# Down projection of the context rows in plain fp32 on four column quarters of the array

## The reference

```python
def expert_choice_ffn(x, w_router, w_gate, w_up, w_down):
    ...
    g, idx = lax.top_k(aff, cap)
    xs = jax.vmap(lambda xb, ib: xb[ib])(x, idx)
    hcur = jax.nn.silu(jnp.einsum('becd,edf->becf', xs, w_gate)) * jnp.einsum('becd,edf->becf', xs, w_up)
    ys = jnp.einsum('becf,efd->becd', hcur, w_down) * g[..., None].astype(x.dtype)
    return jax.vmap(lambda yb, ib: jnp.zeros((n, D), yb.dtype).at[ib.reshape(-1)].add(yb.reshape(-1, D)))(ys, idx)
```

## Time and profile before

| | |
|---|---|
| Median of 3 runs | 3972.54 us (3972.15 to 3976.68) |
| Profiled execution, its own time | 3971.88 us |
| Its span | 3970.1 us |
| Granted TensorE clock, mean | 0.975 |
| Busy PE, PEld, DVE, ACT, POOL | 95%, 85%, 62%, 45%, 12% |
| Expert stage | from about 2200 to 3895 us |

### The profile page before, as it was taken

One profiled execution on the slowest core, in us unless ns is written; L12 is line 12 of the kernel. 1 busy time (PEld: TensorE's weight loads), 2 busy tenths in 40 slices (PEclk: granted clock), 3 DMA queues, 4 the chain that ended last, 5 costly groups with the idle time before them and its releaser, 6 DMA issues. The chain is left out here.

```text
span 3970.1 us, 63525 instructions
## 1 busy us (share of the span) xinstructions
PE 3764.5 (95%) x22936; PEld 3367.7 (85%) x22936; DVE 2455.5 (62%) x4637; ACT 1774.2 (45%) x2654; POOL 472.3 (12%) x517
## 2 busy tenths in 40 slices
PE   8999999999989999999987899999999999999992
PEld 4799999999988888888876788888888888888981
DVE  4745555555566666332225677777777777777774
ACT  3611111111367776311104666666666666665653
POOL 0000000000264644010101000000000000000000
PEclk9999999999999999999998899999999999999996
DMA  9434434433654645645317587888788778888886
GB/s 378 146 129 138 137 124 137 137 130 131 187 168 137 203 144 173 258 144 215 139 40 298 186 259 259 266 264 262 255 275 259 254 261 264 262 263 265 264 251 249
DMA packets 556531, 825.31 MB, mean 208 GB/s; under 512 B 24320, under 2 KB 426144, under 8 KB 544672
## 3 DMA queue, kind: packets, MB, share of 16 engines
q1 hardware_dynamic: 532384, 702.27, 53.4%
q0 software_dynamic: 24064, 121.93, 9.4%
HBM read 717.18 MB, written 108.00 MB: 208 GB/s over the span
## 5 line engine op out<-in xcount | busy, mean ns | idle before, releaser
L2159 DVE TENSOR_TENSOR e_wlo<-e_raw,e_whi 128x1024 fp32r<-128x1024 f32 x768 | 905.2, 1219 | 327.2 <-ACT e_whi L2078 323.9
L2296 PE MATMUL ps<-e_xs,e_whi 128*128 128x320 f32 x4096 | 1054.8, 344 | 10.0 <-DVE e_xs L2173 6.9
L2296 PE MATMUL ps<-e_xs,e_wlo 128*128 128x160 f32 x4096 | 934.9, 238 | 0.0
L2078 ACT ACTIVATE e_whi<-e_raw 128x1024 fp32r<-128x1024 f32 x768 | 766.0, 1049 | 284.8 <-DMA e_raw<-in_w_down 106.4
L2296 PEld LDWEIGHTS ps<-e_xs,e_wlo 128*128 128x128 f32 x4096 | 770.3, 191 | 0.7
L2296 PEld LDWEIGHTS ps<-e_xs,e_whi 128*128 128x128 f32 x4096 | 752.8, 188 | 14.4 <-issue 7.3
L2314 PE MATMUL ps<-e_whi,e_h 128*128 128x512 f32 x1024 | 403.1, 394 | 0.9 <-DVE e_h L2199 0.9
L531 PE MATMUL ps<-hhi,p_whi 128*128 128x428 f32 (+1 forms) x1536 | 381.8, 357 | 8.4 <-DVE p_wlo L463 8.4
L481 DVE SCALAR_TENSOR_TENSOR p_acc<-p_modraw,cT,p_acc 128x256 f32<-128x256 f32 x960 | 386.6, 478 | 0.3 <-DMA p_modraw<-in_w_mod 0.3
L531 PE MATMUL ps<-hlo,p_whi 128*128 128x428 f32 (+1 forms) x1536 | 382.4, 357 | 0.0
L531 PE MATMUL ps<-hhi,p_wlo 128*128 128x428 f32 (+1 forms) x1536 | 380.3, 356 | 0.0
(11 more groups left out here) (252 smaller groups left out, 5359.0 us busy)
## 6 DMA issues: line engine op xcount, KB each, us to landing
e_raw<-in_w_gate SPq DMA_DIRECT2D x64, 2048.0 KB, 7.9
e_raw<-in_w_up SPq DMA_DIRECT2D x64, 2048.0 KB, 7.8
e_raw<-in_w_down SPq DMA_DIRECT2D x64, 2048.0 KB, 8.0
p_modraw<-in_w_mod SPq DMA_DIRECT2D x128, 512.0 KB, 3.5
m_raw<-in_w_mod SPq DMA_DIRECT2D x16, 2048.0 KB, 13.3
p_raw<-in_w_in SPq DMA_DIRECT2D x64, 512.0 KB, 4.7
o_raw<-in_w_out SPq DMA_DIRECT2D x16, 2048.0 KB, 9.0
projT<-p_out_st POOLq DMA_DIRECT2D x30, 640.0 KB, 3.8
```

The costliest lines, as they stand in the source:

```text
L2078: nc.scalar.activation(piece(whi, c, q), piece(raw, c, q), ACT.Copy).then_inc(w_hi_made, 1)
L2159: nc.vector.tensor_tensor(piece(wlo, c, q), piece(raw, c, q), piece(whi, c, q).bitcast(F32), ALU.subtract).then_inc(w_lo_made, 1)
L2296: last = nc.tensor.matmul(bank[:, 0:cols], w[:, s, at:at + P], xs[:, k, 0:cols], start=(k == 0 and w is whi), stop=(k == KD - 1 and w is whi))
```

## The change

The context rows' down product is made by plain fp32 matmuls: h_ctx holds the 32 context rows of h unsplit, and the moving operand is raw itself. Feature block k goes to column quarter k % 4 of the array, that is, to output partitions 32 (k % 4) and up, so that bank 5 or 7 ends with four partial sums. ScalarE copies the first into ys_c (copy_first_part), VectorE adds the other three (SUMS counts the steps of the semaphore, NPART is 4). The h tile keeps only latent columns.

The 8 matmuls of a chunk are a call of ctx_rows. Chunks 0 and 1 are called after feature block 3 of chunk 0, chunk 2 after block 5 of chunk 1, chunk 3 after block 5 of chunk 2. A call waits for all 8 blocks of h, for the chunk's weights in raw and for the scaling that frees its bank. Since raw has a second reader, pieces of wlo wait for the calls, and with them the loads.

```diff
-                sp.wait_ge(w_lo_made, e * EP + c * NP + NP)
+                sp.wait_ge(w_lo_made, e * EP + c * NP + (NP + 3 if c == NUP + 2 else NP))
...
-                nc.scalar.activation(h[:, 2 * j + b, 0:CAP], usum[:, b, :], ACT.Copy).then_inc(h_hi, 1)
-
-            def copy_ctx_low(e, d):
-
-                act.wait_ge(piece_used, e * EP + (NUP + d) * NP + NP + SLOTS)
-                nc.scalar.activation(ctx_low[:, d % 2, :], ps[CAP_C:2 * CAP_C, 5 + (d % 2) * 2, :], ACT.Copy
-                                     ).then_inc(ctx_low_copied, 1)
+                nc.scalar.activation(h[:, 2 * j + b, 0:CAP_L], usum[:, b, 0:CAP_L], ACT.Copy).then_inc(h_hi, 1)
+
+            def copy_first_part(e, d):
+
+                act.wait_ge(ctx_multiplied, e * ND + d + 1)
+                if d == 0:
+                    act.wait_ge(scattered, e * 32 + FIRST)
+                nc.scalar.activation(ys_c[:, d * DW:d * DW + DW], ps[0:CAP_C, 5 + (d % 2) * 2, :], ACT.Copy
+                                     ).then_inc(first_part_copied, 1)
...
                 for q in pieces:
+                    if c == NUP + 1 and q == 2:
+                        dve.wait_ge(ctx_multiplied, e * ND + 1)
+                    if c % NCH > NUP and c < NCH and q == 3:
+                        dve.wait_ge(ctx_multiplied, e * ND + (c - NUP + 1))
...
-                nc.vector.tensor_tensor(h[:, 2 * j + b, CAP:CAP + CAP_C], full[:, CAP_L:CAP], hi[:, CAP_L:CAP],
-                                        ALU.subtract)
+                nc.vector.tensor_copy(h_ctx[:, 2 * j + b, :], full[:, CAP_L:CAP])
...
-                dve.wait_ge(ctx_low_copied, e * ND + d + 1)
-                nc.vector.tensor_tensor(ys_c[:, cols], ps[0:CAP_C, bank + 1, :], ctx_low[:, d % 2, :], ALU.add
-                                        ).then_inc(ctx_summed, 1)
-                dve.wait_ge(ctx_summed, e * ND + d + 1)
+                dve.wait_ge(first_part_copied, e * ND + d + 1)
+                for part in range(1, NPART):
+                    nc.vector.tensor_tensor(ys_c[:, cols], ps[part * CAP_C:part * CAP_C + CAP_C, bank + 1, :],
+                                            ys_c[:, cols], ALU.add).then_inc(affinity_or_ctx_sum, 1)
+                    dve.wait_ge(affinity_or_ctx_sum, e * SUMS + 2 + d * (NPART - 1) + part)
...
+            def ctx_rows(e, d):
+
+                c = NUP + d
+                pe.wait_ge(h_lo, e * KF + KF)
+                pe.wait_ge(w_loaded[c % 2], e * (NCH * 8) + (c // 2) * 16 + 16)
+                pe.wait_ge(ys_made, e * (2 * ND) + (2 * (d - 1) if d >= 2 else 0) + AHEAD)
+                bank = 5 + (d % 2) * 2
+                for k in range(KF):
+                    part = k % NPART
+                    last = nc.tensor.matmul(ps[part * CAP_C:part * CAP_C + CAP_C, bank, :], h_ctx[:, k, :],
+                                            raw[:, c % 2, k * DW:k * DW + DW], start=(k < NPART),
+                                            stop=(k >= KF - NPART))
+                last.then_inc(ctx_multiplied, 1)
...
-                            parts = [(h[:, k, CAP_L:CAP + CAP_C], wh, 2 * CAP_C), (h[:, k, CAP_L:CAP], wl, CAP_C)]
-                            for x, w, rows in parts if k < KF - 1 else parts[::-1]:
-                                last = nc.tensor.matmul(bc[0:rows, :], x, w, start=(k == 0 and w is wh),
-                                                        stop=(k == KF - 1 and w is wh))
+                                last = nc.tensor.matmul(bl, x, w, start=(k == 0 and i == 0),
+                                                        stop=(k == KF - 1 and i == 2))
                             if k % 2 == 1:
                                 last.then_inc(piece_used, 1)
+                            if d == 0 and k == 3:
+                                ctx_rows(e, 0)
+                                ctx_rows(e, 1)
+                            if d in (1, 2) and k == 5:
+                                ctx_rows(e, d + 1)
```

More of the change, by code:

```diff
@@ L1953, in experts @@
     TURNS = (range(0, 2), range(2, NGR))
+    NPART = P // CAP_C
+    SUMS = 2 + ND * (NPART - 1)
     XSTEPS = NGR + 1
@@ L1971, in experts @@
     ys_made = sem("e_ys_made")
-    affinity_set = sem("e_affinity_set")
     scattered = sem("e_scattered")
-    ctx_low_copied = sem("e_ctx_low_copied")
-    ctx_summed = sem("e_ctx_summed")
+    first_part_copied = sem("e_first_part_copied")
+    ctx_multiplied = sem("e_ctx_multiplied")
+    affinity_or_ctx_sum = sem("e_affinity_or_ctx_sum")
     with ExitStack() as ctx:
@@ L1985, in experts @@
         usum = sb("e_usum", [P, 2, CAP])
-        h = sb("e_h", [P, KF, 2 * CAP], F32R)
+        h = sb("e_h", [P, KF, 2 * CAP_L], F32R)
         ys_c = sb("e_ys_c", [CAP_C, D])
-        ctx_low = sb("e_ctx_low", [CAP_C, 2, DW])
+        h_ctx = sb("e_h_ctx", [P, KF, CAP_C])
         index_l = sb("e_index_l", [P, 1], U32)
@@ L2131, in expert @@
                     else:
-                        copy_ctx_low(e, c - NUP - 1)
+                        copy_first_part(e, c - NUP - 1)
                     if following:
@@ L2139, in expert @@
                             ctx_high(e + 1)
-                copy_ctx_low(e, ND - 1)
+                copy_first_part(e, ND - 1)
             make_hi(0, 0, range(NP))
@@ L2195, in h_low @@
                 dve.wait_ge(h_hi, e * KF + 2 * j + b + 1)
-                hi, full = h[:, 2 * j + b, 0:CAP].bitcast(F32), usum[:, b, :]
-                nc.vector.tensor_tensor(h[:, 2 * j + b, CAP:CAP + CAP_C], full[:, CAP_L:CAP], hi[:, CAP_L:CAP],
-                                        ALU.subtract)
-                nc.vector.tensor_tensor(h[:, 2 * j + b, CAP + CAP_C:2 * CAP], full[:, 0:CAP_L], hi[:, 0:CAP_L],
+                hi, full = h[:, 2 * j + b, 0:CAP_L].bitcast(F32), usum[:, b, :]
+                nc.vector.tensor_copy(h_ctx[:, 2 * j + b, :], full[:, CAP_L:CAP])
+                nc.vector.tensor_tensor(h[:, 2 * j + b, CAP_L:2 * CAP_L], full[:, 0:CAP_L], hi,
                                         ALU.subtract).then_inc(h_lo, 1)
@@ L2235, in expert @@
                         dve.wait_ge(scattered, e * 32 + FIRST)
-                        nc.vector.tensor_copy(aff_l[:], gL[:, ds(e, 1)]).then_inc(affinity_set, 1)
-                        nc.vector.tensor_copy(aff_c[:], gC[0:CAP_C, ds(e, 1)]).then_inc(affinity_set, 1)
-                        dve.wait_ge(affinity_set, e * 2 + 2)
+                        nc.vector.tensor_copy(aff_l[:], gL[:, ds(e, 1)]).then_inc(affinity_or_ctx_sum, 1)
+                        nc.vector.tensor_copy(aff_c[:], gC[0:CAP_C, ds(e, 1)]).then_inc(affinity_or_ctx_sum, 1)
+                        dve.wait_ge(affinity_or_ctx_sum, e * SUMS + 2)
                     else:
@@ L2302, in expert @@
                         d = c - NUP
-                        bl, bc = (ps[:, 4 + (d % 2) * 2, :], ps[:, 5 + (d % 2) * 2, :])
+                        bl = ps[:, 4 + (d % 2) * 2, :]
                         pe.wait_ge(ys_made, e * (2 * ND) + (2 * (d - 1) if d >= 2 else 0) + AHEAD)
@@ L2311, in expert @@
                             wh, wl = (w[:, s, k * DW:k * DW + DW] for w in (whi, wlo))
-                            hh, hl = h[:, k, 0:CAP_L], h[:, k, CAP + CAP_C:2 * CAP]
+                            hh, hl = h[:, k, 0:CAP_L], h[:, k, CAP_L:2 * CAP_L]
                             for i, (x, w) in enumerate(((hh, wh), (hh, wl), (hl, wh))):
-                                nc.tensor.matmul(bl, x, w, start=(k == 0 and i == 0), stop=(k == KF - 1 and i == 2))
-                            parts = [(h[:, k, CAP_L:CAP + CAP_C], wh, 2 * CAP_C), (h[:, k, CAP_L:CAP], wl, CAP_C)]
-                            for x, w, rows in parts if k < KF - 1 else parts[::-1]:
-                                last = nc.tensor.matmul(bc[0:rows, :], x, w, start=(k == 0 and w is wh),
-                                                        stop=(k == KF - 1 and w is wh))
+                                last = nc.tensor.matmul(bl, x, w, start=(k == 0 and i == 0),
+                                                        stop=(k == KF - 1 and i == 2))
                             if k % 2 == 1:
                                 last.then_inc(piece_used, 1)
+                            if d == 0 and k == 3:
[3 more added lines that the diff above has]
+                                ctx_rows(e, d + 1)
                         if d < 2 and not last_expert:
```

## The result

The changed kernel takes 4240.28 us (median, 4233.61 to 4244.75), the kernel before on the same chip 3972.35 (3969.18 to 3976.68): ratio 1.0669, 95% interval 1.0656 to 1.0683, so 268 us or 16.7 us per expert slower. The profiled execution took 4233.61 us.

The account below looks back on a forecast made before the run. PE was taken to set the pace, 104.5 us per expert, 16 times. The profiled execution's 3971.9 plus 256 us (16.0 per expert, work and waits) plus 62 us of clock gave 4290 us; range 4120 to 4425.

Parts of the forecast that it names:

- rival (a): Context calls: four quarters really run together, 1.7 us a call; 4129 us, or 4170 with clock loss; chance 0.28.
- Removed: Down part on PE: two of five 512-column matmuls go, 14.7 us per expert.
- Added on PE: Context calls: plain fp32 matmuls overlapping in a chain, 3.9 us per chunk, 15.5 per expert; switches 0.6 more.
- The wait for h: Before the first context call: PE waits for all 8 h blocks, 5.9 us per expert (3.9 to 6.3).
- The two for the scaling: Third and fourth context calls: PE waits for VectorE's scaling to free the bank, 4.9 and 2.4 us per expert.
- The start of the next expert: Second gate/up block: VectorE's pieces come late for PE, some 1.8 us more per expert.
- Clock: PE at half speed after the 5.9 and 4.9 us waits, second counted half: 3.9 us per expert, 62 us.
- Rival (d): Expert stage: waits as worked out, but the clock does not fall; 4228 us; chance 0.11.
- (b): Context calls: no overlap at all, 6.9 us a call; 4378 us, or 4420 with clock loss; chance 0.22.
- (c): Down part: quarters together and waits mostly absent; faster if waits total below 7.2 us per expert, at best 3857; chance 0.04.
- starts nearly together in fours: Profile sign in the context calls: instructions starting this way would mean four quarters really run together.
- VectorE's total still fits. Its order does not: VectorE: 80.2 of 104.5 us per expert, so its total fits, but its order makes PE wait.

Follow-up runs that it names:

- without the scatter: Changed kernel with the two transfers adding an expert's rows to y replaced by two one-row transfers: 4200.53 us, ratio 1.0568.
- The filled waits: Changed kernel plus unread matmuls, 14 before the first context call and 26 before the third (none there in the last expert): 4198.79 us, ratio 1.0563.
- the one-quarter run: Changed kernel with all eight matmuls of a context call in column quarter 0: 4478.12 us, ratio 1.1276.
- the order mended: Changed kernel with the down chunks' scaling and sums put ahead of the next block's first two pieces: 4147.18 us, ratio 1.0442.
- no block held, the calls late and one addition: Changed kernel with calls reading context inputs instead of raw, first two calls after the last h block, one VectorE addition per chunk: 3973.43 us, ratio 1.0005.

## Why the prediction was right

Forecast 4290, measured 4240.28, inside the range and inside the forecast's own 4220 to 4340. That it fell into the latter was luck: PE's work was put 7.8 us per expert too high, the waits 1.7 and the clock 2.5 too low. The true case was rival (a), whose waits add up to 17.0 us (5.9 + 7 + 2.2 + 1.9) against 16.7 measured; its 4170 is too low because it counts 2.6 us of clock where there were 6.4. Per expert, for the 16.7 us:

**Removed**, 14.7 us of PE: as forecast. PE's busy time is nearly the same as before (3759.9 against 3764.5) only because half clock puts back what the shorter work saves.

**Added on PE**: here the step failed. "The second of quarter 0 starts with the first of quarter 1, and so on down the chain" gave 3.9 us per call; it is 1.9 at full clock. That puts PE's work at 4 x 1.92 + 0.6 - 14.7 = 6.4 us less, where the forecast had 1.4 more. The quarters' disjoint outputs, which I named as the only thing for rival (a), were enough. Beside it I had set a rule, that starts and ends keep program order across tiles (the Trainium skill, TensorE: Matmul & The Clock Gate, Part 3). It gives 3.9 us only if the two instructions of a matmul are neighbours in that order, which was my assumption; the rows show 1.92. Whether the rule or the assumption fails is open, since no row here shows which instruction of a pair starts when.

**Waits**: right in kind and place, wrong in size. The wait for h is 4.1 us (65.9 over 16; forecast 5.9, bounds 3.9 to 6.3). The two for the scaling make 9.0 (143.3 over 16; forecast 4.9 + 2.4, in (a) 7 + 2.2). The start of the next expert costs 3.6 more (61.5 - 3.2, over 16; forecast 1.8). The forecast has no term for the load that takes some 12 us beside the scatter; without the scatter 1.4 of the 3.6 go (61.5 to 38.7, over 16). In the kernel before that load took 8.9 to 13.0 us in six experts (2400 to 3000 us), and PE's waits for low parts were 3.2 us in all, so it was hidden there. Sum 16.7 against 15.0. One slip in the working: 25.5 + 3.4 is 28.9 and not 29.1, so the second wait of the forecast is 4.7, 3 us less in all.

**Clock**: the rule of cost held, the count did not. What is left of the account, 16.7 + 6.4 - 16.7 = 6.4 us, is PE at half clock, and the clock sum of 6.7 us says so too; the forecast had 3.9. Both large waits have it in full (0.51 in 3378 to 3384; the 3.64 us of the third call), where I had counted half of the second, and the waits at the start of the next expert can have it too (0.50 in 3450 to 3455). The filled waits gave 4 us of it back. Rival (d), no loss of clock, is out.

**Rivals.** (b) is out by the call of 1.92 us, and the one-quarter run gave what it would have been, 4478, above my 4420. (c) was put right: it needed waits below 7.2 us, and they are 13.1 before the calls alone. Of the signs named for the profile, the third load 12.2 us after the first down matmul came as forecast, and starts nearly together in fours pointed to (a). "VectorE's total still fits. Its order does not" held: with the order mended 93 us go. But the total counts as well: eight of its additions cost 98 us here.

## What to carry to other kernels

An engine that is 60% busy on average can have no slack where it releases the buffers of a load stream that runs back to back. In such a stretch count each added microsecond, and each piece whose release is put off, as up to about one of the total: here 5.7 us of VectorE cost 6.1 and 5.0 in the kernels without lead, half clock included, and 5.4 cost 2.8 in the one with it. If a change makes an engine use a buffer for another purpose, follow the release of that buffer to the next load and to the engine that waits for it, before counting the work saved. Price the long waits of the matmul engine twice, as idle time and as half clock behind them (here up to 2.9 us behind waits of 3.3 to 6.4 us). And where sums of a finished block stand behind work on a block that has become late, put them first.

## What was not expected of the hardware

Plain fp32 matmuls, two instructions each, in four column quarters run fully together: 16 instructions in 1.92 us against 7.03 in one quarter. PE's waits of 3.3 to 6.4 us cost it again afterwards in half clock: some 6 us per expert beside 16.7 of idle time. So a change can save time without a microsecond less of waiting: without the scatter the waits only moved, and 40 us went. And saving PE work gained nothing even with no block held, the calls late and one addition: 6.4 us per expert less on PE, 4.6 of waits and 1.8 of half clock more, and the time of the kernel before (3973.43 against 3973.37).
